# Router products moved ahead of the last norm turn, token numbers found by fp32r products, and replication pieces placed in other slots

## What is computed

```
u = rmsnorm(h); proj = u @ w_in
o_a = HGRN2 recurrence, 4 heads of 128
o_b = differential attention, 4 heads of 64, two softmax maps a head, rotary
o_c = forgetting attention, 4 heads of 64
h = h + concat(o_a, o_b, o_c) @ w_out
u = rmsnorm(h)
g_sel = argmax(u @ w_group + b_group)                    # 1 of 4 groups
top_p, top_i = top_k(softmax(router logits of that group), 2)   # 2 of 8 experts
h = h + sum over both of gate * ((silu(u @ w1[e]) * (u @ w3[e])) @ w2[e])
```

## Time and profile before

| | us |
|---|---|
| three executions, median | 3605.45 |
| lowest and highest of them | 3596.30, 3605.89 |
| profiled execution | 3611.68 |
| its span from first to last instruction | 3609.6 |
| TensorE busy | 3199.5 (89%) |
| VectorE busy | 1528.1 (42%) |
| ScalarE busy | 830.3 (23%) |

### The profile page before, as it was taken

The page is one execution under the profiler, slowest core; times in us unless marked ns, Lnnn a source line. Parts: engine busy times, 40 slices in busy tenths (PEclk is TensorE's granted clock), DMA queues, the critical chain, the costliest instruction groups (busy, mean ns, idle before and its releaser), DMA issues.

```text
span 3609.6 us, 50961 instructions
## 1 busy us (share of the span) xinstructions
PE 3199.5 (89%) x16970; PEld 2057.8 (57%) x16970; DVE 1528.1 (42%) x2613; ACT 830.3 (23%) x1915; POOL 167.9 (5%) x239
## 2 busy tenths in 40 slices
PE   7999788898895999999689997888988959999995
PEld 5666456676543555555356664566765435555553
DVE  4666435544324232233356663346543243323334
ACT  4333124432110011111133331244321101111113
POOL 1300000000000000000200000000000000000002
PEclk9999999888796999999889999987988959999997
DMA  5910100001003799999711000000010049999996
GB/s 161 254 43 12 42 12 7 8 7 59 5 35 144 315 409 410 412 410 407 305 35 35 24 23 25 7 7 8 7 59 17 32 164 374 411 413 411 408 410 240
DMA packets 136560, 592.58 MB, mean 164 GB/s; under 512 B 13000, under 2 KB 47816, under 8 KB 119016
## 3 DMA queue, kind: packets, MB, share of 16 engines
q1 hardware_dynamic: 105688, 491.41, 34.5%
q0 software_dynamic: 20400, 72.69, 6.0%
q10 hardware_dynamic: 10336, 26.75, 1.9%
HBM read 524.55 MB, written 66.26 MB: 164 GB/s over the span
## 4 chain that ended last, share of the span: by engine, by line
PE 77%; DVE 11%; issue 6%; ACT 3%; DMA 1%; DVEq 1%; POOL 1%; ACTq 0%; POOLq 0%; SPq 0%
PE ps L1103 7%; PE ps L1495 7%; PE ps L1536 7%; PE ps L1501 7%; PE ps L1526 6%; PE ps L1144 6%; PE ps L1426 6%; PE ps L1237 4%; PE ps L1553 3%; PE ps L1382 3%; PE ps L1199 3%; PE ps L1224 3%; PE ps L1322 2%; PE ps L1305 2%; DVE negmax L1805 1%
## 5 line engine op out<-in xcount | busy, mean ns | idle before, releaser
L1144 PE MATMUL ps<-arena 128*128 128x260 f32 x1024 | 297.2, 424 | 7.7 <-DVE arena L1751 7.4
L1103 PE MATMUL ps<-arena 128*128 128x512 f32 (+1 forms) x768 | 262.8, 501 | 7.5 <-ACTq L578 3.8
L1805 DVE TENSOR_REDUCE negmax<-ps 16x1 f32<-16x16 f32 (+8 forms) x216 | 151.5, 705 | 269.7 <-PE ps L1204 268.8
L799 ACT ACTIVATE arena<-ps,negmax 16x16 f32<-16x16 f32 (+8 forms) x216 | 150.8, 699 | 473.1 <-DVE negmax L1805 467.4
L1495 PE MATMUL ps<-arena 128*128 128x512 f32 x544 | 246.2, 606 | 2.0 <-DVE arena L2282 2.0
L1536 PE MATMUL ps<-arena 128*64 128x256 f32 x2176 | 242.3, 381 | 0.0
L1305 PE MATMUL ps<-arena 128*128 128x256 f32 x1024 | 229.6, 382 | 14.3 <-ACT arena L892 14.3
L1501 PE MATMUL ps<-arena 128*128 128x256 f32 x1088 | 240.4, 379 | 0.0
L1526 PE MATMUL ps<-arena 128*128 128x512 f32 x544 | 239.3, 593 | 0.0
L1501 PEld LDWEIGHTS ps<-arena 128*128 128x128 f32 x1088 | 206.7, 190 | 42.6 <-issue 16.3
L1426 PE MATMUL ps<-arena 128*128 128x512 f32 x512 | 222.4, 592 | 0.0
(11 more groups left out here) (344 smaller groups left out, 4222.1 us busy)
## 6 DMA issues: line engine op xcount, KB each, us to landing
arena<-w SPq DMA_DIRECT2D x204, 2048.0 KB, 12.9
xg<-arena POOLq DMA_DIRECT2D x51, 512.0 KB, 12.3
xg<-arena ACTq DMA_DIRECT2D x34, 512.0 KB, 7.4
arena<-w_in SPq DMA_DIRECT2D x16, 1024.0 KB, 5.7
xg<-arena ACTq DMA_DIRECT2D x68, 128.0 KB, 9.0
arena<-w_in SPq DMA_DIRECT2D x16, 512.0 KB, 4.0
arena<-w_out SPq DMA_DIRECT2D x2, 4096.0 KB, 13.6
u_rows<-arena SPq DMA_DIRECT2D x16, 512.0 KB, 2.6
```

The lines of the kernel that those rows point to most:

```text
L1103: mm = pe.matmul(dst[0:hi - lo, a:b], w[:, k, lo:hi], uT[:, k, a:b], start=(k == 0), stop=(k == KD - 1))
L1144: mm = pe.matmul(out, w_qk[b][:, k, :], uT[:, k, lo:hi], start=(k == 0), stop=(k == KD - 1), skip_group_check=True)
L1805: v.tensor_reduce(negmax[0:r, at:at + 1], flat[0:r, side:side + wide_], AX.X, ALU.max, negate=True)\
```

## The change

Three parts:

1. **Router products.** `logits` multiplies two column halves side by side as before. 784 columns (`EARLY` = 392 a half, tiles 0 to 6) are multiplied in PSUM bank 3 between the turns of tiles 7 and 8; ScalarE copies them (two copies) behind its norm copy of tile 8 and before the meeting. The last 256 columns (128 a half, bank 4) follow the meeting, and two copies. The products of 16 columns are gone.
2. **Token numbers.** Masks and `token_in` move to the fp32r area `rounded`, so each product is one instruction. A token number is given as two halves (number // 32 * 32 and number % 32), so that each is exact; `token_in` is 68 wide. For the 128 large slots: 9 products per choice. For the 64 small slots: both choices' masks side by side, 9 products of 136 columns. VectorE joins the parts with three reductions, a copy and an addition. As `rounded` lies under W2[0] and W1[1], SyncE waits for the first gather (`m_x[0]`) between the issue of W3[0] and that of W2[0].
3. **Plan.** `PLAN_DA` puts the pieces in other slots and banks, for j = 0 to 6 and 8; d0 of the next head moves to the last slot of the step 8 before. `PLAN_FX` and `DURING_V` stay.

```diff
@@ -68,6 +68,7 @@
+EARLY = (META + (T - 3) * P) // 2
@@ -148,15 +149,15 @@
-0: [["b1@6"], ["d0@2"], ["a2.0@1"], ["e0@6"], ["f0@2"], ["a2.1@1"]],
-1: [["c1@6"], [], ["a2.2@1"], ["d1@6"], [], ["e1@6", "a2.3@1"]],
-2: [["g@4"], ["f1@6"], ["b2@2"], [], [], ["c2@6"]],
-3: [["a3.0@2"], ["d2@6"], [], ["e2@6", "a3.1@2"], [], ["f2@6", "a3.2@2"]],
-4: [[], ["a3.3@2"], [], [], ["b3@6"], []],
-5: [["o@6"], ["a0.0@2+"], ["c3@6"], [], ["d3@6", "a0.1@2+"], []],
-6: [["e3@6"], ["a0.2@2+"], ["f3@6"], [], ["h@6", "a0.3@2+"], []],
+0: [["a2.0@1"], ["e0@2"], [], ["f0@6"], ["b1@2"], ["a2.1@1"]],
+1: [[], ["a2.2@1"], ["c1@6"], [], ["d1@2"], ["a2.3@1"]],
+2: [["g@4"], ["e1@6"], [], ["f1@2"], ["b2@6"], []],
+3: [["a3.0@2"], [], ["c2@6"], ["a3.1@2"], ["d2@6"], []],
+4: [["e2@6"], ["a3.2@2"], ["f2@6"], ["a3.3@2"], [], ["b3@6"]],
+5: [["a0.0@2+"], ["o@6"], [], ["c3@6"], ["a0.1@2+"], ["d3@6"]],
+6: [[], ["e3@6", "a0.2@2+"], [], ["f3@6"], ["a0.3@2+"], ["h@6"]],
 7: [[], ["b0@6+"], [], ["a1.0@6+"], [], ["a1.1@6+"]],
-8: [[], ["a1.2@6+"], [], ["a1.3@6+"], ["c0@2+"], []]}
+8: [[], ["a1.2@6+"], [], ["a1.3@6+"], ["c0@2+"], ["d0@6+"]]}
@@ -179,7 +180,7 @@
-out = [(1, "c0@2")] if slot == 0 else []
+out = [(1, "c0@2"), (1, "d0@6")] if slot == 0 else []
@@ -460,8 +462,8 @@
-token_in = s.take(2 * T, ROUNDS + 2)
 ids = [s.take(ROUNDS + 2).bitcast(I32), s.take(ROUNDS + 2).bitcast(I32)]
+id_parts = s.take(3, ROUNDS + 2)
@@ -471,12 +473,17 @@
-chosen = arena[:, s.at:s.at + 2 * T * SPAN].rearrange("p (m n) -> p m n", m=2 * T)
+N_TURN = ROUNDS + 2
+cuts = [0, 2 * T * P, 2 * T * SPAN, 2 * T * SPAN + 4 * T * N_TURN]
+chosen = rounded[:, cuts[0]:cuts[1]].rearrange("p (m n) -> p m n", m=2 * T)
+chosen_small = rounded[:, cuts[1]:cuts[2]].rearrange("p (j k n) -> p j k n", j=T, k=2)
+token_in = rounded[:, cuts[2]:cuts[3]].rearrange("p (j k n) -> p j k n", j=T, k=2)
+in_turn = arena[:, s.at:s.at + T * N_TURN].rearrange("p (j n) -> p j n", j=T)
 sg = s.take(F)
 G = s.take(F)
 GT = s.take(KF, P)
 yb = s.take(2, D)
-assert s.at <= SCRATCH and 2 * T * SPAN <= 2 * F + KF * P + 2 * D
+assert s.at <= SCRATCH and T * N_TURN <= 2 * F
@@ -697,6 +704,9 @@
+
+if k == 0:
+    wait_alone(sp, m_x[0], before * 16 + layer * 32 + 16)
@@ -996,15 +1006,18 @@
+    act.wait_ge(r_lg, ONE + layer * 3 + 1)
+    for c in range(2):
+        act.activation(lgT[0:ROUTES, c * EARLY:(c + 1) * EARLY], ps[64 * c:64 * c + ROUTES, 3, 0:EARLY],
+                       ACT.Copy).then_inc(r_turn, 1)
     meet(act, layer, 4)
 
 
 if stop > 5:
-    act.wait_ge(r_lg, ONE + layer * 3 + 1)
-    act.activation(lgT[0:ROUTES, 0:512], ps[0:ROUTES, 0, :], ACT.Copy).then_inc(r_turn, 1)
-    act.activation(lgT[0:ROUTES, 512:1024], ps[64:64 + ROUTES, 0, :], ACT.Copy).then_inc(r_turn, 1)
     act.wait_ge(r_lg, ONE + layer * 3 + 2)
-    act.activation(lgT[0:ROUTES, 1024:L], ps[0:ROUTES, 1, 0:META], ACT.Copy).then_inc(r_turn, 1)
+    for c in range(2):
+        act.activation(lgT[0:ROUTES, 2 * EARLY + c * P:2 * EARLY + (c + 1) * P],
+                       ps[64 * c:64 * c + ROUTES, 4, 0:P], ACT.Copy).then_inc(r_turn, 1)
@@ -1429,22 +1442,27 @@
+
+    def logits(bank, lo, n):
+
+        for k in range(KD):
+            for c in range(2):
+                mm = pe.matmul(ps[64 * c:64 * c + ROUTES, bank, 0:n], w_r[:, k, :],
+                               uT2[:, k, lo + c * n:lo + (c + 1) * n], start=(k == 0), stop=(k == KD - 1),
+                               skip_group_check=True)
+        mm.then_inc(r_lg, 1)
+
+    pe.wait_ge(r_w, layer * 112 + 112)
+    pe.wait_ge(n_ua[1], ONE + layer * T + T - 2)
+    pe.wait_ge(n_uv[1], ONE + layer * T + T - 2)
+    logits(3, 0, EARLY)
     norm_turn(1, layer, T - 1)
     meet(pe, layer, 4)
 
 
 if stop > 5:
-    pe.wait_ge(r_w, layer * 112 + 112)
-    for k in range(KD):
-        for c in range(2):
-            mm = pe.matmul(ps[64 * c:64 * c + ROUTES, 0, :], w_r[:, k, :],
-                           uT2[:, k, 512 * c:512 * c + 512], start=(k == 0), stop=(k == KD - 1))
-    mm.then_inc(r_lg, 1)
-    for k in range(KD):
-        mm = pe.matmul(ps[0:ROUTES, 1, 0:META], w_r[:, k, :], uT2[:, k, 2 * 512:L],
-                       start=(k == 0), stop=(k == KD - 1))
-    mm.then_inc(r_lg, 1)
-    wait_alone(pe, r_turn, ONE + layer * 3 + 3)
+    logits(4, 2 * EARLY, P)
+    wait_alone(pe, r_turn, ONE + layer * 4 + 4)
@@ -1462,11 +1480,15 @@
-    pe.wait_ge(r_chosen, ONE + layer * 2 + k + 1)
-    for m in range(k * T, (k + 1) * T):
-        for bank, n, at in ((4, P, 0), (6, SMALL, P)):
-            mm = pe.matmul(ps[0:n, bank, 0:ROUNDS + 2], chosen[:, m, at:at + n], token_in[:, m, :],
-                           start=(m == 0), stop=(m == 2 * T - 1))
+    pe.wait_ge(r_chosen, ONE + layer * 4 + 1 + k)
+    for j in range(T):
+        pe.matmul(ps[:, 4, 0:2 * N_TURN], chosen[:, k * T + j, :], token_in[:, j, k, :],
+                  start=(j + k == 0), stop=(j + k == T))
+wait_alone(pe, r_chosen, ONE + layer * 4 + 4)
+for j in range(T):
+    mm = pe.matmul(ps[:, 6, 0:4 * N_TURN], chosen_small[:, j, :, :].rearrange("p k n -> p (k n)"),
+                   token_in[:, j, :, :].rearrange("p k n -> p (k n)"),
+                   start=(j == 0), stop=(j == T - 1))
@@ -2258,17 +2280,30 @@
-    mine, shape = slice(k * T, (k + 1) * T), [P, T, ROUNDS + 2]
-    do(v.tensor_tensor(token_in[:, mine, :], dest_turn[:, k, :].unsqueeze(2).to_broadcast(shape),
-                       in_span[:, 0:ROUNDS + 2].unsqueeze(1).to_broadcast(shape), ALU.is_equal))
-    do(v.tensor_tensor(token_in[:, mine, :], token_in[:, mine, :],
-                       token_no.unsqueeze(2).to_broadcast(shape), ALU.mult))
-    v.tensor_tensor(chosen[:, mine, :], dest_in[:, k, :].unsqueeze(2).to_broadcast([P, T, SPAN]),
-                    in_span.unsqueeze(1).to_broadcast([P, T, SPAN]), ALU.is_equal)\
-     .then_inc(r_chosen, 1)
+    do(v.tensor_tensor(in_turn, dest_turn[:, k, :].unsqueeze(2).to_broadcast([P, T, N_TURN]),
+                       in_span[:, 0:N_TURN].unsqueeze(1).to_broadcast([P, T, N_TURN]), ALU.is_equal))
+    do(v.tensor_tensor(token_in[:, :, k, :].rearrange("p j (a n) -> p j a n", a=2),
+                       in_turn.unsqueeze(2).to_broadcast([P, T, 2, N_TURN]),
+                       token_no.unsqueeze(3).to_broadcast([P, T, 2, N_TURN]), ALU.mult))
+    if k == 0:
+        chosen_now = [(chosen[:, 0:T, :], 0, 0, P)]
+    else:
+        chosen_now = [(chosen[:, T:2 * T, :], 1, 0, P), (chosen_small[:, :, 0, :], 0, P, SMALL),
+                      (chosen_small[:, :, 1, :], 1, P, SMALL)]
+    for out, which, at, n in chosen_now:
+        made = v.tensor_tensor(out, dest_in[:, which, :].unsqueeze(2).to_broadcast([P, T, n]),
+                               in_span[:, at:at + n].unsqueeze(1).to_broadcast([P, T, n]), ALU.is_equal)
+        made.then_inc(r_chosen, 1)
 v.wait_ge(r_named, ONE + layer + 1)
-for k, n, bank in ((0, P, 4), (1, SMALL, 6)):
-    v.tensor_copy(ids[k][0:n], ps[0:n, bank, 0:ROUNDS + 2]).then_inc(r_ids, 1)
+def joined(out, named):
+    do(v.tensor_reduce(out, named.rearrange("p (a n) -> p n a", a=2), AX.X, ALU.add))
+
+joined(id_parts[:, 2, :], ps[:, 4, 0:2 * N_TURN])
+v.tensor_copy(ids[0], id_parts[:, 2, :]).then_inc(r_ids, 1)
+for k in range(2):
+    joined(id_parts[0:SMALL, k, :], ps[k * SMALL:(k + 1) * SMALL, 6, 2 * k * N_TURN:2 * (k + 1) * N_TURN])
+v.tensor_tensor(ids[1][0:SMALL], id_parts[0:SMALL, 0, :], id_parts[0:SMALL, 1, :], ALU.add)\
+ .then_inc(r_ids, 1)
```

16 lines of the change are left out of this document (8 added, 8 removed).

## The result

The changed kernel takes 3542.36 us in the median (3539.47 to 3546.92, four executions), the kernel before beside it 3605.67: a ratio of 0.9832, 95% interval 0.9812 to 0.9851, or 60.6 us less (54 to 68). The ratio is not the quotient of the two medians, which lie 63.3 us apart. A second set of five on another chip gave 3543.64, ratio 0.9837 (0.9809 to 0.9865). The forecast was 3546 and 59.6 us.

A forecast was written before the change was run, and what follows sets the result against it. TensorE bounds the kernel, at reduced clock in attention and routing, pacing the expert rounds at full clock. 2 x (8.0 + 10.3 - 0.5) = 35.6, plus 24, is 59.6 us: 3546 us from the 3605.45 median, range 3520 to 3578.

The forecast's parts named there:

- Edit 1: Router products: most columns fill TensorE's hole before tile 8's turn, so VectorE starts on logits earlier; 8.0 us a layer gained.
- rival (e): Router: early products don't fit the hole or end at half clock, 5 us a layer, 3556; inside the forecast's 0.55.
- Edit 2: Token numbers: 27 products replace 72, 8.5 us (7.3 to 9.0), plus 1.8 from the first gather; 10.3 us a layer.
- that rule: Token-number products: faster non-fp32 weight loads would hide them behind VectorE's masks, gain some 1.7 us a layer larger; not adopted.
- The price on SyncE: Expert rounds: W2[0] and three more transfers wait for the first gather; cost 0 to 1, taken as 0.5 us a layer.
- Under steady load such a gather took 14.3: First rounds: the small gather, the closest case, is needed 13.9 us after issue, against 14.3 under steady load.
- none is late, because the queue's idle stretch before 1198 pays: First two rounds: delayed weights land near G+7 to G+29, before TensorE wants them, G being the first gather's end.
- rival (c): Rounds: prefetch missed, 20.5 us a layer, 3587, chance 0.07 in full; small dose 3.5 a layer, 3553, inside the forecast's spread.
- Edit 3: Attention's replication pieces reordered: 1.6 us of waits and some 2.5 of clock, 4 us a head, 24 in all.
- (a): Attention: waits only move to steps 3 to 6, clock falls later; about 4 us gained in all, 3566; chance 0.20.
- (d): Attention: spaced waits keep the clock at half through steps 3 to 6, +11 us a head, 3635; chance 0.06.
- (b): Attention: the clock stays up from step 0 to step 6, 45 us gained, 3525; chance 0.12.

The follow-up runs named there:

- router, naming and wait kernels: Kernel before with only the early router products (ratio 0.9945), only the one-pass token numbers and SyncE's wait (0.9929), or only that wait (1.0002).
- c2's move: Kernel before with c2 moved from the end of step 2 to step 3, and d2, e2, f2 one place back: 3600.65 us, ratio 0.9986.
- second plan: Changed kernel with a3 pieces earlier, b3 at slot 3 of step 4, steps 4 to 6 looser: 3506.41 us (0.9738), again 3515.31 (0.9741).
- high masks: Changed kernel with masks and token numbers at the fp32r area's upper end, only W3[1] and W2[1] under them: 3537.18 us against 3543.64.

## Why the prediction was right, and where it was not

**The sum.** 59.6 us forecast, 60.6 measured. Its parts, timed alone: 16.0 forecast and 20 (12 to 27) measured for the router, 19.6 and 26 (16 to 36) for the naming, 24 and 17 (12 to 23) for the plan. The forecast lies inside the first two intervals and 1 us outside the third; the sum is closer than its parts, which is luck.

**Edit 1: right.** 8.0 us a layer forecast, 8.1 and 8.4 measured. VectorE's start 3.4 us behind the meeting was the near end (3.4 to 5.2): the last products ran in 1.95 us, and the turn took 1.09, as the earlier trace rows has it for a turn behind a busy engine (1.04). The early products took 5.46 us in the hole where 5.2 was forecast, so rival (e) did not come.

**Edit 2: right in kind, 1 us too small.** The products start 0.213 us apart, less than the 0.25 taken and less than the nearer end, 0.233; the masks came as worked out (1120.2 for the second choice, 5.3 us after the start of 1114.88; 5.5 forecast); and VectorE's idle time was 2.86 where 3 to 4 was said; 9.5 us a layer instead of 8.5. The gather gave 1.3 and 1.9 for 1.8. The weight loads of these products, at half clock:

```profile
L1485 PEld LDWEIGHTS ps<-rounded 128*128 128x128 f32 x18 | 4.0, 328 | 14.8 <-DVE rounded L2294 14.8
```

are no faster than the fp32 loads of the earlier trace rows (310 ns): of either type the single loads take 333 or 286 ns. The Trainium skill (TensorE: Matmul & The Clock Gate, section Weight-path perf modes) has such loads faster; these rows don't show it. The gain was 1.0 us a layer larger than forecast, where that rule gave 1.7, and it came by a shorter pace with the same loads. The loads overlap: in a group each starts 0.213 us after the one before, for 68 columns and for 136, so a load's length was no lower bound for the pace, and both ends of the prediction's range (0.233 and 0.333) were too high.

**The price on SyncE: the failed step.** 0.5 us a layer was taken; the rounds cost 4.1 and 2.0 in the first pair of traces and 1.9 and 5.7 in the second, and 2.3 in the mean of all traces. Two readings of the step fell. "Under steady load such a gather took 14.3": it took 15.2 (issued at 1138.05, 5.2 us behind the gather as forecast, wanted 13.9 later), and TensorE waited 1.47. And "none is late, because the queue's idle stretch before 1198 pays" looked at the first two rounds only, and at when a transfer is late, not at how much lead is left: no weight was late there, but W3[0]'s lead fell from some 6 us to 1 and never came back, and late rounds paid (1.7 us in layer 0, all in rounds 13 to 17). With a share of 1.01 a delay is not over once the first needs are met. This was the small dose of rival (c), named and priced at 3.5 a layer, but put inside the forecast's spread instead of into the sum.

**Edit 3: near in size, by other parts.** Timed alone it gave 17 us (12 to 23) for 24 forecast. The traces give more, with a wide margin. In the eight attentions with the old plan (traces of the kernel before and of the router, naming and wait kernels) the stage took 465.1 to 478.1 us, mean 471.7; in eight with the new one 452.1 to 466.0, mean 459.0: 12.7 a layer, 25 in all, and by their scatter 10 more or less. The part behind the first three heads, whose plan is unchanged, averages 270.5 and 269.5. So 11.6 us a layer lie in the first three heads, 3.9 a head for 4 forecast. Of that, idle time is 7.5 a layer (38.7 to 31.2), 2.5 a head where 1.6 was forecast, and the rest, 1.4 a head for 2.5, is the clock: its stretches at half went from 57.6 to 43.9 us a layer.

The waits that the step named came nearly as priced: d2 1.01 (1.35 forecast), b3 1.21 (1.6), c3 1.5 to 1.7 (1.5), e3 2.2 to 2.4 (2.6), f3 0.3 to 0.7 (0.7), c2 0.14 (0.8). But it left others out. It said that b2 waits for nothing; b2 waits 0.57, and 1.18 in head 0, and b0 in step 7, which the step does not mention, waits 1.54 in heads 0 and 1. In the means of the same sixteen attentions the waits ahead of the replication products fall from 26.0 to 17.2 us a layer and those ahead of b rise from 1.9 to 9.3. What made up for that was not forecast either: waits ahead of the scores fell by 1.6, of the projection pieces by 1.7, of g, h and o by 2.6. That these about cancel against b is luck.

**The rivals.** (a) was wrong in size for this plan, though 7.4 of the 8.8 us that the replication products gave came back ahead of b, and right for a small edit of the old one: c2's move alone gave 5 us (from 11 less to 1 more), because the wait comes back at f2. (c) did not come in full: the wait on SyncE alone cost nothing that the time shows. (d) did not come: waits of 1.0 to 2.4 us some 5 us apart did not hold the clock at half. (b) did not come either; the second plan, with 29% less idle time, still has some 22 us a layer at half clock in the first three heads.

**What stays open.** Whether high masks gain time: some 3 us by all traces, 6 in one pair of medians, -7 in the other. How long the clock is at half behind the first three heads differs between executions of the same instructions (81 to 119 us a layer in the sixteen attentions above); what decides it was not tried. That the plan alone timed 17 us while the traces give 25 lies within that scatter. Whether a plan with both o and c3 free of VectorE's queue exists was not tried further.

**The faster kernel.** The second plan on top of the three edits is the best that ran, at a ratio of 0.974 in both sets, 1.0% below the changed kernel.

## What to carry to other kernels

Follow each reordered piece to the engine that frees its buffer, and go on until the idle time of the whole stretch is counted: a wait removed at one place is a gain only if the sum of waits falls, and a higher clock gives back only what the other engines can feed, nearly half of it lost in one plan here and little in another. Before a clock's rise is put down to an edit, look at what the unchanged order of instructions does in other executions. Where a transfer queue is full in the steady state, price a late start over the whole loop, by the lead that it leaves, not over its first rounds. When a wait goes and time rises, look for the chain that the wait had hidden.

## What the hardware showed that was not expected

- A queue at a share of 1.01 carried a late start to the end of 17 rounds: from the second round on a transfer of 2.1 MB (W2[0]) landed 11.3 to 12.7 us after issue before, and 17.6 to 20.7 in the changed kernel. The Trainium skill (DMA: Bandwidth & Descriptors, section Queues, rings and completion order) says that an engine takes its queues in turn, packet by packet. A gather that is slower but not stopped beside a full weight queue fits that (the small one took 15.2 us with weights queued, the first one without them 4.5); no run here shows the order of the packets.
- Short fp32r products, each with its own load of 128 weights, start 0.213 us apart at half clock, with 68 columns and with 136, while a load's row says 0.33: the loads overlap.
- The same attention code scatters by 13 us from trace to trace (465.1 to 478.1 in eight), by where the clock falls and, against it, by 3.7 us of idle time. A single trace can't size an edit of 4 us a head; eight on each side leave 10 us either way.
